# Two matmul stages take the residual times its column weights, and the norm's factor comes at their evictions

## The chip, the cores and the metric

The kernel runs on one core of a Trainium2 chip. The metric is the device time of one execution in microseconds (us), as the median of three runs. A difference of about 0.2% (6 us here) is the least that a measurement of this kernel can tell from none.

## What is computed

Two transformer-like blocks over T = 256 tokens of D = 2048 features. The change is in the last two parts of the second block: a cross attention to 256 memory tokens and a squared-ReLU MLP, each behind an RMS norm of the running sum `h`:

```python
def rmsnorm_2(x, w):
    xf = x.astype(jnp.float32)
    y = xf * lax.rsqrt(jnp.mean(xf * xf, axis=-1, keepdims=True) + RMS_EPS)
    return (y * w.astype(jnp.float32)).astype(x.dtype)

def squared_relu_mlp(u, w1, w2):
    return jnp.square(jax.nn.relu(u @ w1)) @ w2
...
        h = h + jnp.concatenate([o_dn, o_rw], axis=-1).astype(h.dtype) @ w_out[l]
        h = h + memory_cross_attention(rmsnorm_2(h, xa_norm_w[l]), rmsnorm_2(mem, mem_norm_w[l]),
                                       xa_wq[l], xa_wk[l], xa_wv[l], xa_wo[l])
        h = h + squared_relu_mlp(rmsnorm_2(h, ffn_norm_w[l]), ffn_w1[l], ffn_w2[l])
    return rmsnorm_2(h, final_norm_w)
```

The norm's factor, `rsqrt(mean(x²) + eps)`, is one number per token. Everything is float32 in and out.

## The kernel before

**Layout.** Activations stand transposed in SBUF: features on the 128 partitions, 16 feature tiles, and the 256 tokens in the columns. The running sum is `resid`, 16 tiles of 128x256. A token's factor is therefore a column's factor, the same for all partitions; `rs` (128x256) holds it on every partition.

**A gemm.** Weights come from HBM in slabs of 512 KB (four 128-row tiles by 256 columns), in a ring of four slots `raw`. ScalarE (ACT) rounds a slab to `hi` (line 276), VectorE (DVE) subtracts to get the rest, `lo` (line 312), and TensorE (PE) multiplies. For one slab it runs a group of 8 matmuls of `hi` against 512 columns (line 375; the moving operand is `x`'s rounded half and its rest side by side) and 8 of `lo` against 256 (line 382). A gemm's block is 256 output features: with K = 2048 it has four such groups, with K = 1024 two, with K = 512 one. A block's two PSUM halves are evacuated by ACT (`half`, line 286) and DVE (lines 325 to 343, by the gemm's kind), and there are two PSUM buffers, so block b+2 waits for the eviction of block b.

**The order of the work** is written out by hand in one program for each engine. ACT and DVE run one block ahead with the splits: split block b+1, then evacuate block b. `follows` names the next gemm, whose first slabs are split before the last block's eviction. `after(b)` is called behind each block, `each()` behind each slab.

**The stages around the change**, in order, with their blocks and groups per block: `g_ob` (w_out, adds to `resid`, 8 x 2), norm 6, `g_xq` (xa_q, stored in `work`, 2 x 4), the attention (`xat_*`), `g_xo` (xa_o, adds to `resid`, 8 x 1), norm 7, `ff2[0]` (w1_0, 8 x 4), then w2_0, w1_1 and so on to w2_3 (ff2 has four w1 gemms, 32 blocks). The w1 gemms are of kind "relu2": their eviction makes `xb` from relu² in four DVE operations.

**A norm here.** While `g_ob` or `g_xo` runs, ACT squares each finished pair of `resid` tiles (`squares_beside`, line 406), GpSimd (POOL) sums them in `sq_sum` (line 440), and behind the last block two more pairs are squared. Then one PE matmul sums over the partitions (`norm_total`, line 449), ACT makes `rs` (Ln, then a table load and Exp, lines 421 and 422), and DVE and ACT write the 16 tiles of `xa` in turns: `half` = resid x weight x rs on DVE (471), its rounding on ACT (454), the rest on DVE (476). PE's first block of the next gemm waits, group by group, for four tiles each (`x_ready`).

Of the kernel before, what the change touches and what calls it, by code (L numbers as in the profile page):

```python
# [7 lines left out]
F32 = mybir.dt.float32  # L8
# [73 lines left out]
class Gemm:  # L82
# [1 line left out]

    def __init__(self, plan, name, w, k, n0, n, x, kind, dst, x_from=0, bias=None, k0=0, apart=P):
        self.name, self.w, self.n0, self.x, self.kind, self.dst = name, w, n0, x, kind, dst
        self.k0, self.x_from, self.bias, self.apart = k0, x_from, bias, apart
# [43 lines left out]
def build_program(nc, a, out):  # L133
# [3 lines left out]
    with ctx:  # L137
# [10 lines left out]
        def sem(name):  # L148
            return ctx.enter_context(nc.semaphore(name))
# [58 lines left out]
        half_out = sem("half_out")  # L208
        evacuated = sem("evacuated")
        summed = sem("summed")  # L210
        squared, rounded = sem("squared"), sem("rounded")
# [105 lines left out]
        def evacuate(dve, g, i, v):  # L317
            t = i * g.unroll + v
            par = (g.b0 + v) % 2
            into, tile, off = g.dst  # L320
            dve.wait_ge(half_out, g.b0 + t + 1)
            psum = pg[:, par, :, 0:T]
            place = into[:, bass.ds(tile + 2 * t, 2), off:off + T]
            if g.kind == "store":
                nc.vector.tensor_tensor(place, psum, half[:, :, :], ALU.add).then_inc(evacuated, 1)  # L325
                return
            own = g.sum0 + t + 1
            if g.kind in ("add", "mult"):
                nc.vector.tensor_tensor(half[:, :, :], psum, half[:, :, :], ALU.add).then_inc(summed, 1)  # L329
                dve.wait_ge(summed, own)  # L330
                nc.vector.tensor_tensor(place, place, half[:, :, :],  # L331
                                        ALU.add if g.kind == "add" else ALU.mult).then_inc(evacuated, 1)
                return
            own_sq = g.sq0 + t + 1
            nc.vector.tensor_tensor(sq[:, :, :], psum, half[:, :, :], ALU.add).then_inc(summed, 1)
            dve.wait_ge(summed, own)
            nc.vector.scalar_tensor_tensor(out=sq[:, :, :], in0=sq[:, :, :], scalar=0.0, in1=sq[:, :, :],
                                           op0=ALU.max, op1=ALU.mult).then_inc(squared, 1)
# [19 lines left out]
        def gemm_pe(pe, g, after=None, x_tiles=None, of=None, each=None):  # L358
# [30 lines left out]
            if x_tiles is not None or of:  # L389

                for v in range(g.unroll):
                    block(0, v, waits=(v == 0))
                    if after:
                        after(v)
                rest = g.blocks - g.unroll
                run_blocks(pe, rest, g.unroll, lambda i, v: block(i + 1, v),
                           (lambda t: after(t + g.unroll)) if after else None)
            else:
                run_blocks(pe, g.blocks, g.unroll, block, after, each)

# [294 lines left out]
        g_xq = Gemm(plan, "xa_q", a["xa_wq_2"], D, 0, 512, xa, "store", (work, 8, PAD))  # L695
        g_xo = Gemm(plan, "xa_o", a["xa_wo_2"], 512, 0, D, xb, "add", (resid, 0, 0))
        ff2 = []
        for p in range(FF_PIECES):
            ff2 += [Gemm(plan, f"w1_{p}", a["ffn_w1_2"], D, p * D, D, xa, "relu2", (xb, 0, 0)),
                    Gemm(plan, f"w2_{p}", a["ffn_w2_2"], D, 0, D, xb, "add", (resid, 0, 0), k0=p * D)]  # L700

        def over(name, shape, region, byte):
# [1011 lines left out]
        def _(act):  # L1714
# [44 lines left out]
            gemm_act(act, g_ob, squares_beside(act, g_ob, 6, resid, 0, 0), follows=g_xq)  # L1759
            norm_act(act, 6, resid, 0, 0, lambda e, k: blocks_out(e, g_ob), DT - 2)  # L1760
            norm_split_act(act, 4, xa)
            gemm_act(act, g_xq, follows=g_xo)
            xat_act(act)
            gemm_act(act, g_xo, squares_beside(act, g_xo, 7, resid, 0, 0), follows=ff2[0])
            norm_act(act, 7, resid, 0, 0, lambda e, k: blocks_out(e, g_xo), DT - 2)
            norm_split_act(act, 5, xa)
            for g, n in zip(ff2, ff2[1:] + [None]):
                gemm_act(act, g, squares_beside(act, g, 8, resid, 0, 0) if g is ff2[-1] else None, follows=n)
            norm_act(act, 8, resid, 0, 0, lambda e, k: blocks_out(e, ff2[-1]), DT - 2)

        @block.vector
        def _(dve):
# [69 lines left out]
        def _(pe):  # L1842
# [78 lines left out]
```

## Time and profile before

| what | value |
|---|---|
| median of 3 runs | 3098.55 us (3097.56 to 3099.07) |
| the profiled execution: its own time | 3098.79 us |
| its span in the profile | 3097.0 us |
| PE busy | 2885.4 us, 93% |
| DVE busy | 1971.7 us, 64% |
| ACT busy | 1446.5 us, 47% |
| POOL busy | 74.0 us, 2% |
| HBM traffic | 156 GB/s over the span |

The span runs from the first to the last instruction; the execution's own time has 1.8 us around it. Busy shares are means over all stages, so what a change in one stage is worth is read from that stage.

### The profile page before, as it was taken

Reading aid. Unit: us, or ns where it says so; the run is one execution under the profiler, and the core shown is the slowest. Engines: PE = TensorE matmul, PEld = TensorE weight load, DVE = VectorE, ACT = ScalarE, POOL = GpSimd, SP = SyncE. Lnnn points to the kernel's source line nnn. Section 1 sums busy time; section 2 is a strip of 40 time slices with the busy share of each in tenths; the row PEclk is TensorE's granted clock in tenths of the full one; section 3 lists DMA queues with packets and bytes.
Section 4 is the critical chain, followed back from the end, with each engine's and each line's share of the span. In section 5 each row is a group of like instructions: output and inputs, shape, how many; then the busy total and the mean of one; then the engine's idle time right before and its main releaser. Section 6 shows DMA issues by size and latency. Waiting matters only on the chain.

```text
span 3097.0 us, 51788 instructions
## 1 busy us (share of the span) xinstructions
PE 2885.4 (93%) x19568; PEld 2514.7 (81%) x19568; DVE 1971.7 (64%) x2513; ACT 1446.5 (47%) x1866; POOL 74.0 (2%) x90
## 2 busy tenths in 40 slices
PE   6999999979999999997998996887968999999997
PEld 5888888868888888886877885776856888888886
DVE  4588886656556565657865566546657656565665
ACT  4445656554444444445476335325435444444443
POOL 0000000010000000010000000000102000000001
PEclk9999999989999999998999997999988999999999
DMA  5655554636565666653644341013624666666664
GB/s 173 184 186 173 168 172 136 202 114 183 188 186 189 186 190 188 188 186 108 190 155 132 116 123 41 3 43 95 197 75 149 187 188 188 189 186 190 185 192 132
DMA packets 480985, 484.50 MB, mean 156 GB/s; under 512 B 14736, under 2 KB 479632, under 8 KB 480704
## 3 DMA queue, kind: packets, MB, share of 16 engines
q1 hardware_dynamic: 480288, 479.01, 50.0%
q0 software_dynamic: 544, 3.38, 0.3%
q8 instruction: 105, 1.72, 0.2%
q14 instruction: 48, 0.39, 0.0%
HBM read 480.23 MB, written 2.10 MB: 156 GB/s over the span
## 4 chain that ended last, share of the span: by engine, by line
PE 43%; DVE 6%; ACT 3%; issue 1%; POOL 0%; DMA 0%; ACTq 0%; POOLq 0%; DVEq 0%; SPq 0%
PE pg L375 24%; PE pg L382 12%; DVE lo L312 1%; PE p L783 1%; PE p L797 1%; PE p L800 1%; PE p L1156 1%; DVE rw_xx L849 0%; ACT hi L276 0%; PE p L459 0%; POOL sq_sum L440 0%; DVE half L487 0%; DVE dnc L884 0%; PE p L1397 0%; DVE resid L331 0%
## 5 line engine op out<-in xcount | busy, mean ns | idle before, releaser
L312 DVE TENSOR_TENSOR lo<-raw,hi 128x1024 fp32r<-128x1024 f32 x904 | 1100.2, 1231 | 818.4 <-ACT hi L276 814.5
L276 ACT ACTIVATE hi<-raw 128x1024 fp32r<-128x1024 f32 x904 | 947.2, 1058 | 1165.5 <-PE pg L382 1160.3
L375 PE MATMUL pg<-xa,hi 128*128 128x512 f32 x4608 | 1174.7, 397 | 38.7 <-DVE xa L476 37.0
L375 PEld LDWEIGHTS pg<-xa,hi 128*128 128x128 f32 x4608 | 835.9, 190 | 198.9 <-issue 44.4
L375 PE MATMUL pg<-xb,hi 128*128 128x512 f32 x2624 | 664.7, 395 | 10.6 <-DVE xb L579 2.9
L382 PEld LDWEIGHTS pg<-xa,lo 128*128 128x128 f32 x4608 | 631.4, 191 | 46.0
L382 PE MATMUL pg<-xa,lo 128*128 128x256 f32 x4608 | 644.5, 283 | 0.0
L375 PEld LDWEIGHTS pg<-xb,hi 128*128 128x128 f32 x2624 | 475.7, 190 | 99.0 <-ACT hi L276 4.4
L382 PEld LDWEIGHTS pg<-xb,lo 128*128 128x128 f32 x2624 | 358.8, 191 | 28.3 <-DVE lo L312 2.4
L382 PE MATMUL pg<-xb,lo 128*128 128x256 f32 x2624 | 366.7, 283 | 2.0 <-DVE lo L312 2.0
L286 ACT ACTIVATE half<-pg 128x512 f32<-128x512 f32 x212 | 123.7, 583 | 83.8 <-PE pg L382 83.8
L505 DVE SCALAR_TENSOR_TENSOR work<-u,vec,work 128x256 f32<-128x256 f32 x240 | 116.2, 484 | 7.6
L329 DVE TENSOR_TENSOR half<-pg,half 128x512 f32<-128x512 f32 x96 | 65.8, 686 | 41.6 <-ACT half L286 41.3
L459 PE MATMUL p<-sq,cst 128*128 128x256 f32 x128 | 45.3, 487 | 33.1 <-ACT sq L406 32.5
L440 POOL TENSOR_TENSOR sq_sum<-sq_sum,sq 128x256 f32<-128x256 f32 x75 | 67.7, 902 | 204.8 <-ACT sq L406 198.6
L325 DVE TENSOR_TENSOR work<-pg,half 128x512 f32<-128x512 f32 (+1 forms) x88 | 60.2, 684 | 11.9 <-ACT half L286 11.9
L459 PEld LDWEIGHTS p<-sq,cst 128*128 128x128 f32 x128 | 24.0, 227 | 53.3 <-ACT sq L406 29.4
L471 DVE SCALAR_TENSOR_TENSOR half<-resid,vec,rs 128x256 f32<-128x256 f32 x80 | 38.4, 485 | 21.0 <-ACT rs L422 18.5
L454 ACT ACTIVATE xa<-half 128x256 fp32r<-128x256 f32 x80 | 33.3, 417 | 36.2 <-DVE half L471 36.2
L813 ACT ACTIVATE rw_tt<-p 128x256 f32<-128x256 f32 (+1 forms) x48 | 18.4, 384 | 67.0 <-PE p L783 56.5
L343 DVE TENSOR_TENSOR xb<-sq,xb 128x512 f32 (+1 forms) x64 | 44.3, 692 | 7.8 <-DVE xb L340 0.9
L331 DVE TENSOR_TENSOR resid<-resid,half 128x512 f32 (+1 forms) x56 | 42.1, 752 | 5.8 <-DVE half L329 4.9
(364 smaller groups left out, 1649.8 us busy)
## 6 DMA issues: line engine op xcount, KB each, us to landing
raw<-w_in SPq DMA_DIRECT2D x264, 512.0 KB, 4.6
raw<-ffn_w SPq DMA_DIRECT2D x256, 512.0 KB, 4.0
raw<-w_up SPq DMA_DIRECT2D x128, 512.0 KB, 3.9
raw<-w_down SPq DMA_DIRECT2D x128, 512.0 KB, 4.4
raw<-w_o SPq DMA_DIRECT2D x32, 512.0 KB, 4.5
raw<-w_out SPq DMA_DIRECT2D x32, 512.0 KB, 3.5
raw<-w_sb_out SPq DMA_DIRECT2D x16, 512.0 KB, 4.7
raw<-w_conv_out SPq DMA_DIRECT2D x16, 512.0 KB, 4.7
```

The source lines that it names most:

```text
L276: nc.scalar.activation(hi[:, slot], raw[:, slot], ACT.Copy).then_inc(hi_ready, 1)
L286: nc.scalar.activation(half[:, :, :], pg[:, par, :, T:2 * T], ACT.Copy).then_inc(half_out, 1)
L312: nc.vector.tensor_tensor(lo[:, slot], raw[:, slot], hi[:, slot].bitcast(F32), ALU.subtract).then_inc(lo_ready, 1)
L325: nc.vector.tensor_tensor(place, psum, half[:, :, :], ALU.add).then_inc(evacuated, 1)
L329: nc.vector.tensor_tensor(half[:, :, :], psum, half[:, :, :], ALU.add).then_inc(summed, 1)
L331: nc.vector.tensor_tensor(place, place, half[:, :, :], ALU.add if g.kind == "add" else ALU.mult).then_inc(evacuated, 1)
L343: nc.vector.tensor_tensor(rest, sq[:, :, :], place.bitcast(F32), ALU.subtract).then_inc(evacuated, 1)
L375: nc.tensor.matmul(pg[:, par, t, :], lhsT=hi[:, slot, k, c:c + P], rhs=g.x[:, kk, :], start=(j == 0 and k == 0), stop=False)
L382: ins = nc.tensor.matmul(pg[:, par, t, 0:T], lhsT=lo[:, slot, k, c:c + P], rhs=g.x[:, kk, 0:T], start=False, stop=(j == g.groups - 1 and k ...
L440: ins = nc.gpsimd.tensor_tensor(sq_sum[:, :], sq_sum[:, :], sq[:, k % 2], ALU.add)
L459: ins = nc.tensor.matmul(ps[0][:, 0:T], lhsT=const("ones"), rhs=sq[:, k % 2], start=(k == 0), stop=(k == DT - 1))
L505: ins = nc.vector.scalar_tensor_tensor(out=acc, in0=x, scalar=v1("w_dw", 8 * j + c), in1=acc, op0=ALU.mult, op1=ALU.add)
```

## The change

The moving operand of `g_xq` and of the w1 gemms becomes `resid` times its column weights alone. Its two halves are written by one ACT operation (`gained_act`, Copy with the weight as scale) and one DVE operation (`gained_dve`) per tile, beside `g_ob` and `g_xo`: ACT handles tiles 2b-2 and 2b-1 behind block b, DVE tiles 2b-4 and 2b-3, and the last ones behind the gemm (two on ACT; six on DVE, those of block 7 counted). The factor `rs` is applied at the evictions of `g_xq` and of all four w1 gemms, by one DVE operation more per block. PE's sum and ACT's root move into the next gemm: `each()` runs them behind its second slab. GpSimd's and SP's programs stay as they are, and so do the DMAs.

```diff
+            if g.kind == "normed":
+                nc.vector.tensor_tensor(half[:, :, :], psum, half[:, :, :], ALU.add).then_inc(summed, 1)
+                dve.wait_ge(summed, own)
+                norm_rs_dve(dve, g.norm)
+                nc.vector.tensor_tensor(place, half[:, :, :], rs[:, None, :].to_broadcast([P, 2, T]),
+                                        ALU.mult).then_inc(evacuated, 1)
+                return
...
+            if g.norm is None:
+                nc.vector.scalar_tensor_tensor(out=sq[:, :, :], in0=sq[:, :, :], scalar=0.0, in1=sq[:, :, :],
+                                               op0=ALU.max, op1=ALU.mult).then_inc(squared, 1)
+            else:
+                norm_rs_dve(dve, g.norm)
+                nc.vector.scalar_tensor_tensor(out=sq[:, :, :], in0=sq[:, :, :], scalar=0.0,
+                                               in1=rs[:, None, :].to_broadcast([P, 2, T]), op0=ALU.max,
+                                               op1=ALU.mult).then_inc(scaled, 1)
+                dve.wait_ge(scaled, own_sq - ff2[0].sq0)
+                nc.vector.tensor_tensor(sq[:, :, :], sq[:, :, :], sq[:, :, :], ALU.mult).then_inc(squared, 1)
...
+        def gained_act(act, n, m, gain, k):
+            nc.scalar.activation(xa[:, k, 0:T], resid[:, k], ACT.Copy, scale=gain(k)).then_inc(norm_hi, 1)
+            square_tile(act, n, k, resid, 0, 0)
+
+        def gained_beside_act(act, g, n, m, gain):
+
+            def after(b):
+                if b:
+                    act.wait_ge(evacuated, g.b0 + b + 2)
+                    for k in (2 * b - 2, 2 * b - 1):
+                        gained_act(act, n, m, gain, k)
+            return after
+
+        def gained_rest_act(act, g, n, m, gain):
+            act_link(nc.scalar.activation(small[:, 140:141], const("ones")[:, 0:1], ACT.Ln))
+            blocks_out(act, g)
+            for k in (DT - 2, DT - 1):
+                gained_act(act, n, m, gain, k)
+
+        def root_later(act, n):
+            yield
+            norm_root(act, n)
+            yield
+
+        def total_later(pe, n):
+            yield
+            norm_total(pe, n)
+            yield
+
+        def gained_dve(dve, m, gain, k):
+            dve.wait_ge(norm_hi, DT * m + k + 1)
+            nc.vector.scalar_tensor_tensor(out=xa[:, k, T:2 * T], in0=resid[:, k], scalar=gain(k),
+                                           in1=xa[:, k, 0:T].bitcast(F32), op0=ALU.mult,
+                                           op1=ALU.subtract).then_inc(x_ready, 1)
+
+        def gained_beside_dve(dve, m, gain):
+
+            def after(b):
+                if b >= 2:
+                    for k in (2 * b - 4, 2 * b - 3):
+                        gained_dve(dve, m, gain, k)
+            return after
...
-            gemm_act(act, g_xo, squares_beside(act, g_xo, 7, resid, 0, 0), follows=ff2[0])
-            norm_act(act, 7, resid, 0, 0, lambda e, k: blocks_out(e, g_xo), DT - 2)
-            norm_split_act(act, 5, xa)
+            gemm_act(act, g_xo, gained_beside_act(act, g_xo, 7, 5, ffn_gain), follows=ff2[0])
+            gained_rest_act(act, g_xo, 7, 5, ffn_gain)
+            root = root_later(act, 7)
...
-            gemm_dve(dve, g_xo, follows=ff2[0])
-            norm_rs_dve(dve, 7)
-            norm_split_dve(dve, 5, xa, resid, 0, 0, lambda k: v2("ffn_norm_w_2", k), 112)
+            gemm_dve(dve, g_xo, gained_beside_dve(dve, 5, ffn_gain), follows=ff2[0])
+            for k in range(DT - 4, DT):
+                gained_dve(dve, 5, ffn_gain, k)
...
-            norm_total(pe, 7)
-            gemm_pe(pe, ff2[0], x_tiles=112)
+            gemm_pe(pe, ff2[0], x_tiles=112, each=step_of(total_later(pe, 7)))
```

`g_xq` has the same three edits with norm 6.

PE's order at the start of `g_xq`, before; the first row is the norm's sum over partitions, the others are the groups of block 0 (the start of `ff2[0]` reads alike):

```order
L449 MATMUL p<-sq_sum,cst 128x256
L375 MATMUL pg<-xa,hi 128x512 x8
L382 MATMUL pg<-xa,lo 128x256 x8
L375 MATMUL pg<-xa,hi 128x512 x8
L382 MATMUL pg<-xa,lo 128x256 x8
L375 MATMUL pg<-xa,hi 128x512 x8
```

The same place after the change (the lines are now 464, 390 and 397):

```order
L390 MATMUL pg<-xa,hi 128x512 x8
L397 MATMUL pg<-xa,lo 128x256 x8
L390 MATMUL pg<-xa,hi 128x512 x8
L397 MATMUL pg<-xa,lo 128x256 x8
L464 MATMUL p<-sq_sum,cst 128x256
L390 MATMUL pg<-xa,hi 128x512 x8
```

The sum has moved behind two groups of matmuls; PE's queue is in order, so the third group stands behind it.

DVE's order at the end of `g_xo`, before: two blocks, the four splits of w1_0's first slabs, the last eviction, and the start of the turns of norm 7:

```order
L331 TENSOR_TENSOR resid<-resid,half 128x512
L312 TENSOR_TENSOR lo<-raw,hi 128x1024
L329 TENSOR_TENSOR half<-pg,half 128x512
L331 TENSOR_TENSOR resid<-resid,half 128x512
L312 TENSOR_TENSOR lo<-raw,hi 128x1024 x4
L329 TENSOR_TENSOR half<-pg,half 128x512
L331 TENSOR_TENSOR resid<-resid,half 128x512
L471 SCALAR_TENSOR_TENSOR half<-resid,vec,rs 128x256 x2
L476 TENSOR_TENSOR xa<-half,xa 128x256
```

The same place after:

```order
L331 TENSOR_TENSOR resid<-resid,half 128x512
L502 SCALAR_TENSOR_TENSOR xa<-resid,vec,xa 128x256 x2
L312 TENSOR_TENSOR lo<-raw,hi 128x1024
L329 TENSOR_TENSOR half<-pg,half 128x512
L331 TENSOR_TENSOR resid<-resid,half 128x512
L502 SCALAR_TENSOR_TENSOR xa<-resid,vec,xa 128x256 x2
L312 TENSOR_TENSOR lo<-raw,hi 128x1024 x4
L329 TENSOR_TENSOR half<-pg,half 128x512
L331 TENSOR_TENSOR resid<-resid,half 128x512
L502 SCALAR_TENSOR_TENSOR xa<-resid,vec,xa 128x256 x6
```

Two operations of line 502 stand behind the eviction of each block from the third on, and six behind the last one; the 32 operations of lines 471 and 476 are gone.

## Rows read from the trace of the kernel before

**Rows 1.** The page's part 4: the chain that ended last, by engine.

```profile
PE 43%; DVE 6%; ACT 3%; issue 1%; POOL 0%; DMA 0%; ACTq 0%; POOLq 0%; DVEq 0%; SPq 0%
```

**Rows 2.** PE's waits over the whole span: in total us, times, longest.

```profile
PE pg L375 <- DVE xa L476: 37.0, 5, 11.9
...
PE p L449 <- POOL sq_sum L440: 31.7, 5, 8.6
```

**Rows 3.** Timeline, `g_ob` to the attention: start us, us, engine, operation.

```profile
2249.22 4.03 DVE L312 TENSOR_TENSOR lo<-raw,hi 128x1024 fp32r<-128x1024 f32 x3
...
2251.45 1.11 PE L382 MATMUL pg<-xb,lo 128*128 128x256 f32 x8
...
2254.59 4.03 POOL L440 TENSOR_TENSOR sq_sum<-sq_sum,sq 128x256 f32<-128x256 f32 x4 [4.69 <-ACT sq L406]
...
2255.61 0.69 DVE L331 TENSOR_TENSOR resid<-resid,half 128x512 f32<-128x512 f32 x1
...
2258.67 1.22 PE L449 MATMUL p<-sq_sum,cst 128*128 128x256 f32 x2 [6.11 <-POOL sq_sum L440]
...
2262.08 0.88 DVE L471 SCALAR_TENSOR_TENSOR half<-resid,vec,rs 128x256 f32<-128x256 f32 x2 [5.77 <-ACT rs L422]
...
2266.19 3.74 PE L375 MATMUL pg<-xa,hi 128*128 128x512 f32 x8 [6.29 <-DVE xa L476]
...
2287.48 2.00 PE L375 MATMUL pg<-xa,hi 128*128 128x512 f32 x8
...
2291.10 0.69 DVE L325 TENSOR_TENSOR work<-pg,half 128x512 f32<-128x512 f32 x1 [6.63 <-ACT half L286]
```

**Rows 4.** Timeline, `g_xo` to the second block of w1_0.

```profile
2339.86 2.11 PE L375 MATMUL pg<-xb,hi 128*128 128x512 f32 x8
...
2342.86 2.10 PE L375 MATMUL pg<-xb,hi 128*128 128x512 f32 x8
...
2344.80 1.11 PE L382 MATMUL pg<-xb,lo 128*128 128x256 f32 x8
...
2345.65 5.16 DVE L312 TENSOR_TENSOR lo<-raw,hi 128x1024 fp32r<-128x1024 f32 x4
...
2350.37 4.07 POOL L440 TENSOR_TENSOR sq_sum<-sq_sum,sq 128x256 f32<-128x256 f32 x4 [4.05 <-ACT sq L406]
...
2351.45 0.69 DVE L331 TENSOR_TENSOR resid<-resid,half 128x512 f32<-128x512 f32 x1
...
2362.01 3.63 PE L375 MATMUL pg<-xa,hi 128*128 128x512 f32 x8 [6.29 <-DVE xa L476]
...
2374.88 2.00 PE L375 MATMUL pg<-xa,hi 128*128 128x512 f32 x8
```

**Rows 5.** Windows in g_ob, g_xo, w1_0: busy PE, PEld, DVE, ACT, POOL; PEclk.

```profile
2208.00:2252.60 44.60, 44.57 (x256) 39.03 (x254) 33.02 (x32) 24.49 (x37) 10.42 (x12) 1.00 0.53 168
...
2321.30:2345.90 24.60, 24.56 (x128) 20.95 (x128) 19.64 (x22) 15.30 (x27) 11.49 (x12) 0.94 0.44 131
...
2375.00:2455.00 80.00, 80.00 (x458) 70.28 (x457) 52.02 (x58) 34.69 (x37) 0.00 (x0) 1.00 0.65 199
```

**Rows 6.** Groups by form, DVE, 2329:2346, in `g_xo`.

```profile
L312 DVE TENSOR_TENSOR lo<-raw,hi 128x1024 fp32r<-128x1024 f32 x7 | 11.5, 1648 | 0.1
```

**Rows 7.** The page's part 5: the splits of line 312, all of them.

```profile
L312 DVE TENSOR_TENSOR lo<-raw,hi 128x1024 fp32r<-128x1024 f32 x904 | 1100.2, 1231 | 818.4 <-ACT hi L276 814.5
```

**Rows 8.** ACT's operation with a per-partition operand: ns min/median/max.

```profile
L1275 ACT ACTIVATE rw_d<-work,vec x8: 494/496/499, 1881.2 to 1884.0; 128x256 f32<-128x256 f32 x8
```

**Rows 9.** Timeline, PE, at two waits of an earlier stage, norms of `g_dn`.

```profile
1580.29 2.07 PE L917 MATMUL p<-sq,cst 128*128 128x512 f32 x2 [2.68 <-ACT sq L931]
1581.37 3.51 PE L375 MATMUL pg<-xa,hi 128*128 128x512 f32 x8
...
1595.41 1.12 PE L917 MATMUL p<-sq,cst 128*128 128x512 f32 x2 [1.20 <-ACT sq L931]
1596.45 2.06 PE L375 MATMUL pg<-xa,hi 128*128 128x512 f32 x8
```

More of the change, by code:

```diff
@@ L82, with __init__ @@
 class Gemm:
-    def __init__(self, plan, name, w, k, n0, n, x, kind, dst, x_from=0, bias=None, k0=0, apart=P):
+    def __init__(self, plan, name, w, k, n0, n, x, kind, dst, x_from=0, bias=None, k0=0, apart=P, norm=None):
         self.name, self.w, self.n0, self.x, self.kind, self.dst = name, w, n0, x, kind, dst
-        self.k0, self.x_from, self.bias, self.apart = k0, x_from, bias, apart
+        self.k0, self.x_from, self.bias, self.apart, self.norm = k0, x_from, bias, apart, norm
         self.groups = k // (P * KG)
@@ L210, in build_program @@
         summed = sem("summed")
-        squared, rounded = sem("squared"), sem("rounded")
+        squared, rounded, scaled = sem("squared"), sem("rounded"), sem("scaled")
         x_ready = sem("x_ready")
@@ L336, in evacuate @@
             dve.wait_ge(summed, own)
-            nc.vector.scalar_tensor_tensor(out=sq[:, :, :], in0=sq[:, :, :], scalar=0.0, in1=sq[:, :, :],
-                                           op0=ALU.max, op1=ALU.mult).then_inc(squared, 1)
+            if g.norm is None:
[8 more added lines that the diff above has]
+                nc.vector.tensor_tensor(sq[:, :, :], sq[:, :, :], sq[:, :, :], ALU.mult).then_inc(squared, 1)
             dve.wait_ge(squared, own_sq)
@@ L396, in gemm_pe @@
                 run_blocks(pe, rest, g.unroll, lambda i, v: block(i + 1, v),
-                           (lambda t: after(t + g.unroll)) if after else None)
+                           (lambda t: after(t + g.unroll)) if after else None, each)
             else:
@@ L454, in norm_split_act @@
                 nc.scalar.activation(x[:, k, 0:T], tmp[:, k % 2], ACT.Copy).then_inc(norm_hi, 1)
+        def gained_act(act, n, m, gain, k):
[32 more added lines that the diff above has]
+            return after
+        xa_gain, ffn_gain = lambda k: v2("xa_norm_w_2", k), lambda k: v2("ffn_norm_w_2", k)
         def norm_pe(pe, n, k0=0, k1=DT):
@@ L694, in build_program @@
         g_ob = Gemm(plan, "w_out rw", a["w_out_2"], D // 2, 0, D, xb, "add", (resid, 0, 0), x_from=8, k0=D // 2)
-        g_xq = Gemm(plan, "xa_q", a["xa_wq_2"], D, 0, 512, xa, "store", (work, 8, PAD))
+        g_xq = Gemm(plan, "xa_q", a["xa_wq_2"], D, 0, 512, xa, "normed", (work, 8, PAD), norm=6)
         g_xo = Gemm(plan, "xa_o", a["xa_wo_2"], 512, 0, D, xb, "add", (resid, 0, 0))
@@ L698, in build_program @@
         for p in range(FF_PIECES):
-            ff2 += [Gemm(plan, f"w1_{p}", a["ffn_w1_2"], D, p * D, D, xa, "relu2", (xb, 0, 0)),
+            ff2 += [Gemm(plan, f"w1_{p}", a["ffn_w1_2"], D, p * D, D, xa, "relu2", (xb, 0, 0), norm=7),
                     Gemm(plan, f"w2_{p}", a["ffn_w2_2"], D, 0, D, xb, "add", (resid, 0, 0), k0=p * D)]
@@ L1758, in _ @@
             gemm_act(act, g_mv, follows=g_ob)
[L1759 to L1762, printed above, removed]
+            gemm_act(act, g_ob, gained_beside_act(act, g_ob, 6, 4, xa_gain), follows=g_xq)
+            gained_rest_act(act, g_ob, 6, 4, xa_gain)
+            root = root_later(act, 6)
+            gemm_act(act, g_xq, follows=g_xo, each=step_of(root))
             xat_act(act)
-            gemm_act(act, g_xo, squares_beside(act, g_xo, 7, resid, 0, 0), follows=ff2[0])
-            norm_act(act, 7, resid, 0, 0, lambda e, k: blocks_out(e, g_xo), DT - 2)
-            norm_split_act(act, 5, xa)
+            gemm_act(act, g_xo, gained_beside_act(act, g_xo, 7, 5, ffn_gain), follows=ff2[0])
+            gained_rest_act(act, g_xo, 7, 5, ffn_gain)
+            root = root_later(act, 7)
             for g, n in zip(ff2, ff2[1:] + [None]):
-                gemm_act(act, g, squares_beside(act, g, 8, resid, 0, 0) if g is ff2[-1] else None, follows=n)
+                gemm_act(act, g, squares_beside(act, g, 8, resid, 0, 0) if g is ff2[-1] else None, follows=n,
+                         each=step_of(root) if g is ff2[0] else None)
             norm_act(act, 8, resid, 0, 0, lambda e, k: blocks_out(e, ff2[-1]), DT - 2)
@@ L1825, in _ @@
             gemm_dve(dve, g_mv, follows=g_ob)
-            gemm_dve(dve, g_ob, follows=g_xq)
-            norm_rs_dve(dve, 6)
-            norm_split_dve(dve, 4, xa, resid, 0, 0, lambda k: v2("xa_norm_w_2", k), 96)
+            gemm_dve(dve, g_ob, gained_beside_dve(dve, 4, xa_gain), follows=g_xq)
+            for k in range(DT - 4, DT):
+                gained_dve(dve, 4, xa_gain, k)
             gemm_dve(dve, g_xq, follows=g_xo)
             xat_dve(dve)
-            gemm_dve(dve, g_xo, follows=ff2[0])
-            norm_rs_dve(dve, 7)
-            norm_split_dve(dve, 5, xa, resid, 0, 0, lambda k: v2("ffn_norm_w_2", k), 112)
+            gemm_dve(dve, g_xo, gained_beside_dve(dve, 5, ffn_gain), follows=ff2[0])
+            for k in range(DT - 4, DT):
+                gained_dve(dve, 5, ffn_gain, k)
             for g, n in zip(ff2, ff2[1:] + [None]):
@@ L1879, in _ @@
             gemm_pe(pe, g_ob)
-            norm_total(pe, 6)
-            gemm_pe(pe, g_xq, x_tiles=96)
+            gemm_pe(pe, g_xq, x_tiles=96, each=step_of(total_later(pe, 6)))
             blocks_out(pe, g_mv)
```

## The prediction

> **What bounds the kernel now.** I read the chain that ended last first: of the engines PE has by far the largest share [rows 1]. PE's own waits come next, since what PE waits for is what could be won: the norms stand among the largest, with 37.0 us in 5 waits for the first tiles of `xa` and 31.7 us in 5 waits for POOL's sums [rows 2]. Then I read the timeline across the two norms that the change touches.
>
> First gap, `g_ob` to `g_xq` [rows 3]: PE's last group ends at 2251.45 + 1.11 = 2252.56. The last block is in `resid` at 2255.61 + 0.69 = 2256.30, POOL has its last sum at 2254.59 + 4.03 = 2258.62, `rs` lets DVE begin at 2262.08, and PE restarts at 2266.19. That is 13.6 us, and the first `hi` group then takes 3.74 us where the later one takes 2.00.
>
> Second gap, `g_xo` to w1_0 [rows 4]: PE ends at 2344.80 + 1.11 = 2345.91 and restarts at 2362.01, 16.1 us, with a first group of 3.63. Here the stage before is not bound by PE alone: its last blocks start 3.00 us apart (2339.86, 2342.86), while a group takes 44.60 / 16 = 2.79 us in `g_ob` [rows 5] (8 matmuls of each kind per group, 256 records). In that stretch a split of 128x1024 on DVE takes 1.648 us [rows 6] against a mean of 1.231 over the kernel [rows 7], with POOL 11.49 us busy in it, and DVE works 19.64 of 24.60 us [rows 5], the early blocks being looser. So DVE sets the pace of `g_xo`'s second half.
>
> **The change, part by part.** Positions are those of the trace before; I walk each gap anew.
>
> *Beside `g_ob`.* DVE's two new operations per block are like the pair at 2262.08, 0.88 us [rows 3]. DVE is busy 33.02 of 44.60 us, 4.13 per block of 5.58 [rows 5]; 5.0 still fits. ACT gains two copies with a per-partition scale; the nearest row, same shape, is 0.496 us [rows 8]. ACT is busy 24.49 of 44.60, 3.1 per block; 4.1 fits. The cover is PE's 5.58 us; without it the block would cost up to 0.9 us more. I take nothing.
>
> *First gap.* PE runs two groups at once: their tiles 0 to 7 and slabs are ready. It is free at 2252.56 + 5.58 = 2258.14 and comes to the norm's sum. What is late now is POOL. DVE's splits start 0.88 later, at 2250.10, three end at 2254.13 (4.03), the fourth at 2255.36 (1.23), the eviction at 2255.36 + 1.40 = 2256.76 (two operations of 0.69). POOL ended 2.32 after `resid` before; one copy in front of the square makes it 2.82: 2259.6. PE waits 1.4 us, behind it the third group and all after it. The sum itself took 1.22 us before, behind a long idle [rows 3]; at the full clock I halve that to 0.61. These are its bounds, and which of them holds hangs on the clock. The clock: behind an idle 1.20 us the matmuls ran 1.12 and 2.06 us, behind 2.68 us they ran 2.07 and 3.51 [rows 9]. 1.4 is nearer to the first, so I take the full clock: 0.61. Six groups follow from 2260.2: 16.74, to 2276.95. Before, the same point was 2287.48 + 2.79 = 2290.27 [rows 3]. Gain 13.3. `g_xq`'s last eviction gets one multiplication, and the attention waits for it: 0.69 as L325 [rows 3], nothing covers it. **Net 12.6 us.** The factor itself (Ln, table load, Exp on ACT) was ready 2.2 us behind the sum's end before, 2258.67 + 1.22 to 2262.08 [rows 3], so here near 2262.4. The first eviction that needs it comes with block 0's end at 2265.8: hidden. Queued behind the root on ACT is the third `hi` of block 1, which can't start before PE's third group ends at 2263.0 anyway.
>
> *Beside `g_xo`.* DVE has no slack here. Each block from the third on costs 0.88 us. Before the splits of w1_0 there are five such pairs: 4.4 us. PE's first group of w1_0 needs the PSUM of block 6, which is four pairs later.
>
> *Second gap* [rows 4]. The splits start at 2345.65 + 4.4 = 2350.05 and take 5.16: 2355.21. PE's first group waits for the first of them, 2350.05 + 1.65 = 2351.7, ends at 2352.7; the second at 2355.5. The last eviction was done 6.49 us behind the start of the splits (2352.14), so 2356.54. POOL was done 2.30 later (2350.37 + 4.07); with the copy 2.80: 2359.34. PE has then idled 3.9 us, more than the 2.68 of the slow row, so the sum is at the low clock, 1.22: 2360.56. Two groups remain, 5.58, and the slow first one adds 3.63 - 2.00 = 1.63: block 1 starts at 2367.8 instead of 2374.88. **Net 7.1 us.**
>
> *The w1 gemms.* Per block DVE gets one more operation of 0.69 and a link of about 0.15: 0.84, 32 times, 27 us of work. DVE is busy 52.02 of 80.00 us in w1_0, 7.3 of a block's 11.16 [rows 5], so 3.9 are free: nothing. Where w2 begins, its fourth group is the one that needs w1's last eviction, and it comes 8.4 us behind w1's end, with the splits and a 2.5 us eviction in front: the 0.84 is hidden there too. Without that cover the four hand-overs would cost 3.4 us.
>
> *Loops.* PE's and ACT's w1_0 is now written out. No row tells a written-out gemm from a looped one in pace; nothing.
>
> **The sum:** 12.6 + 7.1 = 19.7. From the profiled execution's own 3098.79 (span 3097.0 and 1.8 around it) this gives 3079.1; it stands 0.24 above the median, so 3079 for the median.
>
> **A page against the trace.** In `g_xo` a split beside POOL takes 0.42 us more than the mean [rows 6, 7]; I leave that surcharge as it is, since POOL does the same two additions per block. The Trainium skill, SBUF — State Buffer, section "Who interferes with whom", says that a VectorE instruction with two SBUF inputs and a GpSimd one that reads SBUF exclude each other for the whole instruction. The new operation has two such inputs; read to its end this is rival C. The trace agrees in that the splits stretch, and shows no full blocking of each.
>
> **The rivals.**
> A. The clock falls in the first gap too, if POOL is later by half a microsecond or the clock is quicker to fall than the rows show. Price 0.61 + 1.63 = 2.2: 3081.
> B. It does not fall in the second gap: 3077.
> C. VectorE and GpSimd lock each other out at the new operations. POOL is busy 11.49 / 12 = 0.96 us per addition [rows 5], two per block 1.9, of which 0.42 is paid: 1.5 more. Five blocks of `g_xo`: 7.5, 3086.6. In `g_ob` DVE would need 4.13 + 0.88 + 1.5 = 6.5 of 5.58, another 0.9 in six blocks: 3092. For it: the surcharge. Against: it was 0.42, not 1.9.
> D. It does not close the gaps: if PE's first groups effectively wait for DVE's last tile (2256.76 + six operations of 0.44 = 2259.4; 2359.2 in the second), the gains are about 2290.27 - (2259.4 + 22.3 + 2.2) - 0.7 = 5.7 and 2374.88 - (2359.2 + 11.2 + 2.8) = 1.7: 3091. Against: `x_ready` is asked for four tiles at a time, and tile 7 is written in block 5's turn.
> E. Slower: the w1 evictions become the bound. From the point where the added DVE work per block passes the 3.9 us free, or a lateness of block b reaches PE's block b+2, each of 32 blocks pays 0.84: 27 us against the gain of 19.7, 3106. For it: it is the only part repeated 32 times. Against: the free 3.9.
>
> **How the numbers follow.** Forecast 62% (its own range 3077 to 3082), A 15, B 8, C 8, D 4, E 2, 1 unnamed. The range 3075 to 3086 holds the forecast, A and B and the lower part of C; half a microsecond of POOL either way and a pair at 0.80 to 1.0 us instead of 0.88 move the sum by 2. Faster by over 0.2% (below 3092): forecast, A, B, nearly all of C and D, 0.94. Within 0.2%: the rest of C and D, 0.04. Slower: 0.02.
>
> **What the profile after would show.** First gap: PE's waits for `xa` fall from 5 to 3; one wait of 1 to 2 us for POOL in `g_xq` with the next group at 2.0 to 2.1 us (3.5: rival A). `g_xo`: blocks some 3.9 us apart from the fourth on (over 4.5: C). Second gap: a wait of about 4 us for POOL, then a slow group. w1: DVE busier, groups still 2.79 us apart; any wait of PE for an eviction there speaks for E. The prediction is wrong if the L502 operations take clearly over 0.5 us, or if POOL's last sum comes later than 3 us behind the last eviction.

## The result

The changed kernel takes 3079.84 us as the median of four runs (3077.72 to 3080.55), against 3098.06 for the kernel before on the same chips: a ratio of 0.9941, with a 95% interval of 0.9929 to 0.9954. That is 18.2 us less; 19.7 were forecast, at 3079 in a range of 3075 to 3086.

### The profile page after: what moved, and what is told of

Same layout as the page of the kernel before. It is cut to its first block, busy times and chain, and to the rows that moved or that the text cites. A ratio compares the mean times of both kernels' runs of the same rounds, so it can differ in the third digit from the quotient of the medians.

```text
span 3075.9 us, 51736 instructions
## 1 busy us (share of the span) xinstructions
PE 2884.0 (94%) x19568; PEld 2512.2 (82%) x19568; DVE 1982.4 (64%) x2515; ACT 1446.2 (47%) x1866; POOL 78.4 (3%) x90
## 4 chain that ended last, share of the span: by engine, by line
PE 43%; DVE 6%; ACT 3%; issue 1%; POOL 0%; ACTq 0%; DVEq 0%; POOLq 0%
PE pg L390 24%; PE pg L397 12%; DVE lo L312 1%; PE p L843 1%; PE p L857 1%; PE p L860 1%; PE p L1216 1%; DVE rw_xx L909 0%; ACT hi L276 0%; PE p L519 0%; DVE half L547 0%; DVE resid L331 0%; DVE dnc L944 0%; DVE half L329 0%; PE p L1457 0%
## 5 line engine op out<-in xcount | busy, mean ns | idle before, releaser
L390 PEld LDWEIGHTS pg<-xb,hi 128*128 128x128 f32 x2624 | 475.4, 190 | 100.2 <-ACT hi L276 5.3
L421 ACT ACTIVATE sq<-resid 128x256 f32<-128x256 f32 x96 | 38.5, 411 | 16.3 <-PE p L519 8.9
L331 DVE TENSOR_TENSOR resid<-resid,half 128x512 f32<-128x512 f32 (+1 forms) x56 | 41.5, 741 | 5.0 <-DVE half L329 3.9
L342 DVE TENSOR_TENSOR sq<-pg,half 128x512 f32<-128x512 f32 x64 | 43.8, 684 | 0.0
```

What stands on the lines that cost most here:

```text
L390: nc.tensor.matmul(pg[:, par, t, :], lhsT=hi[:, slot, k, c:c + P], rhs=g.x[:, kk, :], start=(j == 0 and k == 0), stop=False)
```

## The profile after

The profiled execution of the changed kernel is the fastest of its four (3077.72, span 3075.9). PE's waits over the whole span, in total, times and longest, which answer to [rows 2]:

```profile
PE pg L390 <- DVE xa L536: 24.5, 3, 11.9
PE p L464 <- POOL sq_sum L455: 22.1, 5, 6.1
```

The waits for tiles of `xa` have gone from 5 to 3, and the rest are those of other norms. The waits for POOL are still 5, but shorter.

The timeline from the end of `g_ob` to the attention, which answers to [rows 3]:

```profile
2248.36 4.62 DVE L312 TENSOR_TENSOR lo<-raw,hi 128x1024 fp32r<-128x1024 f32 x4
...
2249.05 1.12 PE L397 MATMUL pg<-xb,lo 128*128 128x256 f32 x8
...
2253.62 0.69 DVE L331 TENSOR_TENSOR resid<-resid,half 128x512 f32<-128x512 f32 x1
2254.23 3.88 DVE L502 SCALAR_TENSOR_TENSOR xa<-resid,vec,xa 128x256 fp32r<-128x256 f32 x6
...
2255.66 1.77 POOL L455 TENSOR_TENSOR sq_sum<-sq_sum,sq 128x256 f32<-128x256 f32 x2 [0.76 <-ACT sq L421]
...
2257.48 0.70 PE L464 MATMUL p<-sq_sum,cst 128*128 128x256 f32 x2 [1.73 <-POOL sq_sum L455]
...
2257.83 2.20 PE L390 MATMUL pg<-xa,hi 128*128 128x512 f32 x8
...
2276.33 0.69 DVE L338 TENSOR_TENSOR work<-half,rs 128x512 f32<-128x512 f32 x1
...
2277.17 5.38 PE L1692 MATMUL p<-work 128*128 128x256 f32 x16 [2.23 <-DVE work L338]
...
2282.59 2.29 DVE L1724 TENSOR_REDUCE small<-p 128x8 f32<-128x2048 f32 x1 [5.56 <-PE p L1692]
```

Read it from PE. `g_ob` ends at 2249.05 + 1.12 = 2250.17, and two groups of `g_xq` follow at once. PE then waits 1.73 us for POOL, whose last addition ends at 2255.66 + 1.77 = 2257.43, 3.1 us behind the last eviction (2254.31). The sum takes 0.70 us and the next group 2.20: the clock stayed up, as forecast. At the end stands something that was not forecast: the attention's 16 score records take 5.38 us. In the kernel before, the same row, behind the eviction that ends [rows 3], was:

```profile
2291.94 3.69 PE L1632 MATMUL p<-work 128*128 128x256 f32 x16 [1.50 <-DVE work L325]
```

The windows of these two rows, the changed kernel's first; the third number from the end is the granted clock:

```profile
2277.17:2282.55 5.38, 5.38 (x18) 4.37 (x19) 0.00 (x0) 0.00 (x0) 0.00 (x0) 0.68 0.00 0
2291.94:2295.63 3.69, 3.69 (x18) 3.23 (x19) 0.00 (x0) 0.00 (x0) 0.00 (x0) 1.00 0.00 0
```

PE waited 2.23 us for them instead of 1.50, because `g_xq`'s eviction has one operation more (L338), and they run 1.7 us longer: 1.00 is TensorE's full clock, 2.4 GHz, and part of the 5.38 us ran at its lower level of 1.2.

The same for `g_xo` and w1_0, which answers to [rows 4]:

```profile
2308.26 3.68 PE L390 MATMUL pg<-xb,hi 128*128 128x512 f32 x8 [2.65 <-DVE xb L1737]
...
2318.71 1.27 DVE L312 TENSOR_TENSOR lo<-raw,hi 128x1024 fp32r<-128x1024 f32 x1 [0.94 <-ACT hi L276]
...
2328.91 2.09 PE L390 MATMUL pg<-xb,hi 128*128 128x512 f32 x8 [0.19 <-DVE resid L331]
...
2332.64 2.11 PE L390 MATMUL pg<-xb,hi 128*128 128x512 f32 x8 [0.19 <-DVE resid L331]
...
2337.44 4.62 DVE L312 TENSOR_TENSOR lo<-raw,hi 128x1024 fp32r<-128x1024 f32 x4
...
2342.70 0.69 DVE L331 TENSOR_TENSOR resid<-resid,half 128x512 f32<-128x512 f32 x1
...
2344.38 1.73 POOL L455 TENSOR_TENSOR sq_sum<-sq_sum,sq 128x256 f32<-128x256 f32 x2 [0.40 <-ACT sq L421]
...
2346.16 1.22 PE L464 MATMUL p<-sq_sum,cst 128*128 128x256 f32 x2 [3.44 <-POOL sq_sum L455]
...
2346.82 3.35 PE L390 MATMUL pg<-xa,hi 128*128 128x512 f32 x8
...
2350.94 2.00 PE L390 MATMUL pg<-xa,hi 128*128 128x512 f32 x8
...
2353.74 2.00 PE L390 MATMUL pg<-xa,hi 128*128 128x512 f32 x8
```

`g_xo`'s late blocks start 3.73 us apart (2328.91, 2332.64) instead of 3.00: DVE's two new operations per block cost 0.73 net. Ahead of the first such pair DVE also starts a split late (2318.71, 10.45 us behind the first row; 9.50 before): the new copies on ACT had pushed that slab's `hi` back. The splits of w1_0 start 29.18 us behind the first row, 4.9 us later than before. PE waits 3.44 us for POOL, runs the sum with the next group 0.66 us behind its start, and that group is slow (3.35 us; 4.12 to the next start instead of 2.79). Block 1 of w1_0 is the last row, 2353.74.

DVE's new operation over the whole kernel (ns, minimum/median/maximum), and then the windows of `g_ob`, `g_xo` and w1_0, which answer to [rows 5]:

```profile
L502 DVE SCALAR_TENSOR_TENSOR xa<-resid,vec,xa x32: 470/950/968, 2224.2 to 2346.7; 128x256 fp32r<-128x256 f32 x32
```

```profile
2208.00:2250.00 42.00, 42.00 (x243) 36.96 (x242) 35.33 (x40) 26.89 (x47) 11.75 (x12) 1.00 0.56 175
2308.30:2337.40 29.10, 27.40 (x133) 21.71 (x134) 23.18 (x31) 21.01 (x40) 13.91 (x12) 0.94 0.39 118
2356.50:2436.50 80.00, 80.00 (x458) 70.32 (x457) 56.60 (x66) 34.19 (x36) 0.00 (x0) 1.00 0.60 186
```

The operation takes 0.95 us in the middle, twice what I had assumed, though in `g_xo` only one of each pair does; the sum was still right to a microsecond, and the experiments show why. In w1_0 DVE has gone from 52.0 to 56.6 us of 80, and PE has no gap in it.

To compare profiled executions I cut each trace at four marks on PE, the same in every kernel: the end of `g_ob`, the first score, the first group of `g_xo`, and the start of w1_0's block 1. What lies ahead of the first mark differs between executions although the programs are alike there: the changed kernel's is 2.4 us shorter (2252.56 to 2250.17), which is why its span is 21.1 us shorter and its median only 18.2.

| kernel | median us (before, same chip) | end of g_ob to scores | scores to g_xo | g_xo to block 1 of w1_0 | sum |
|---|---|---|---|---|---|
| before | 3098.06 | 39.38 | 29.40 | 53.54 | 122.3 |
| changed | 3079.84 (3098.06) | 27.00 | 31.09 | 45.48 | 103.6 |
| e1_xq_only | 3087.72 (3097.21) | 26.98 | 31.09 | 53.76 | 111.8 |
| e2_w1_only | 3089.91 (3097.21) | 39.38 | 29.40 | 45.19 | 114.0 |
| e4_store_xq | 3078.62 (3097.21) | 26.27 | 29.17 | 46.81 | 102.3 |
| e5_transposes_first | 3076.10 (3097.21) | 26.90 | 29.29 | 43.98 | 100.2 |
| e7_w1_no_factor | 3078.79 (3098.63) | 26.98 | 31.09 | 45.48 | 103.6 |
| e6_pool_fills | 3077.88 (3098.63) | 26.23 | 32.12 | 43.73 | 102.1 |
| e3_sum_late | 3073.29 (3098.63) | 25.20 | 29.40 | 43.94 | 98.5 |
| e8_both | 3073.51 (3098.63) | 25.13 | 27.74 | 42.40 | 95.3 |
| e9_late_and_sooner | 3068.98 (3098.06) | 25.00 | 27.71 | 40.17 | 92.9 |
| e10_all_three | 3067.87 (3098.06) | 24.92 | 27.74 | 40.16 | 92.8 |

From the last mark to the end all twelve take 722.0 to 722.3 us. The medians of e4 to e7 differ from the changed kernel's by less than the 6 us that a measurement can tell from none. Of the variants e3 to e10 only e9 and e10 have an interval of the ratio to the kernel before that lies clear of the changed kernel's 0.9929 to 0.9954; those of e3 (0.9907 to 0.9934) and e8 (0.9906 to 0.9933) just meet it. What the smaller steps are worth is read from the marks, which are one execution each.

## The experiments

**Each half alone.** In e1_xq_only norm 7 and the w1 gemms go back to the old form:

```diff
-            gemm_pe(pe, ff2[0], x_tiles=112, each=step_of(total_later(pe, 7)))
+            norm_total(pe, 7)
+            gemm_pe(pe, ff2[0], x_tiles=112)
```

> Only g_xq takes the weighted residual (norm 6 as in the changed kernel, norm 7 and the w1 gemms as before). The theory from the changed kernel's trace: the first gap is worth 12.4 us between the end of g_ob and the attention's first matmul, and 1.7 us of it is given back because those matmuls run 5.38 us instead of 3.69. So 10.7 us under the kernel before, near 3087.4. Rival: the two gaps are not independent, the greater part comes from the w1 side and from the loops written out there; then this run is less than 8 us under the kernel before, over 3090.

In e2_w1_only norm 6 and `g_xq` do:

```diff
-            gemm_pe(pe, g_xq, x_tiles=96, each=step_of(total_later(pe, 6)))
+            norm_total(pe, 6)
+            gemm_pe(pe, g_xq, x_tiles=96)
```

> Only the w1 gemms take the weighted residual (norm 7 as in the changed kernel, norm 6 and g_xq as before). The theory: the trace puts 8.1 us on this part, against 7.1 in the prediction; near 3090.0, with the attention's first matmuls at 3.7 us as before. Rival: 7.1 or less was right and the rest is spread between executions, 3091 or more. With the other half the two gains add up to 18 to 19 us.

Measured: 9.5 us under the kernel before (0.9968, 0.9955 to 0.9980) and 7.3 us under it (0.9976, 0.9966 to 0.9985). Together 16.8 against 18.2 for both. The marks add up more closely: 10.5 and 8.4 us, against 18.7. So the two parts add up, within what the executions of one kernel differ by, the first gap is worth more than the second, and the first part brings its slow scores along (31.09 in the second column).

**Whose are the slow scores?** e4_store_xq evicts `g_xq` without the factor:

```diff
-        g_xq = Gemm(plan, "xa_q", a["xa_wq_2"], D, 0, 512, xa, "normed", (work, 8, PAD), norm=6)
+        g_xq = Gemm(plan, "xa_q", a["xa_wq_2"], D, 0, 512, xa, "store", (work, 8, PAD))
```

> The changed kernel, with g_xq evicted by the one addition as before: the factor of norm 6 is left out of the result, and one DVE operation of 0.69 us goes from each of its two evictions. Theory: PE's idle time before the attention falls from 2.2 to 1.5 us, its clock then stays up, the 16 records of the scores take 3.7 instead of 5.4 us, and the run is 0.7 + 1.7 = 2.4 us under the changed kernel, 3077.4. Rival: the slow scores come from the wait for POOL inside g_xq or from chance; then they stay near 5.4 us and the run is only 0.7 us under, 3079.1.

PE's timeline, the scores and then `g_xo`'s first and fourth group:

```profile
2277.83 3.69 PE L1692 MATMUL p<-work 128*128 128x256 f32 x16 [1.50 <-DVE work L325]
...
2307.00 3.78 PE L390 MATMUL pg<-xb,hi 128*128 128x512 f32 x8 [2.65 <-DVE xb L1737]
...
2318.71 2.11 PE L390 MATMUL pg<-xb,hi 128*128 128x512 f32 x8 [0.26 <-ACT hi L276]
```

Waiting 1.50 us, the scores are at full pace again (granted clock 1.00), and the first two columns are 2.65 us shorter. The last one gave 1.3 us back in this execution (46.81 instead of 45.48), since `g_xo` began with a longer slow stretch: from its first to its fourth group 11.7 us, against 10.5 in the changed kernel. The median is 1.2 us under the changed kernel's, with intervals that overlap. The place is shown by the trace, the size of it in the median is not settled.

e5_transposes_first keeps the factor and gives PE work to do meanwhile:

```diff
-            blocks_out(pe, g_xq)
-            for h in range(XA_H):
...
-            XA_.pe.done(ins, "s")
+            pe.wait_ge(evacuated, g_xq.b0 + 3)
             for n in range(8):
                 ins = nc.tensor.transpose(pgq(0)[:, n], chunk(4 + n // 2, n % 2), const("ident"))
             XA_.pe.done(ins, "v")
+            blocks_out(pe, g_xq)
+            for h in range(XA_H):
...
+            XA_.pe.done(ins, "s")
```

> The changed kernel, with the attention's eight transposes of v put ahead of the scores, so that PE has 1.04 us of work while g_xq's last eviction runs. Theory of the clock by idle time: PE idles some 1.2 us before the scores, they take 3.7 us, and with the transposes out of the way the run is up to 1.7 us under the changed kernel (DVE waits for the scores alone, so hiding the transposes gives nothing by itself), 3078.1. Rival: eight short transposes don't keep the clock, the scores stay at 5.4 us and the run is the same as the changed kernel, 3079.8.

PE's rows, transposes, scores, and the first group of `g_xo`:

```profile
2276.27 1.04 PE L1691 MATMUL pg<-cst,work 128*128 128x128 f32 x8
2278.57 3.72 PE L1696 MATMUL p<-work 128*128 128x256 f32 x16 [1.26 <-DVE work L338]
...
2307.86 2.10 PE L390 MATMUL pg<-xb,hi 128*128 128x512 f32 x8 [2.65 <-DVE xb L1738]
```

The scores are at full pace behind 1.26 us, as expected. The last row was not expected: behind the same 2.65 us of waiting as in all other kernels so far, that group took 2.10 us, not 3.5 to 3.8. The marks are 3.4 us shorter, the sum of both (1.8 in the second column, 1.5 in the third). The median is 3.7 us under the changed kernel's, 2.0 more than the forecast of up to 1.7; the intervals of the ratios overlap (0.9918 to 0.9945 here).

**Where the sum stands.** e3_sum_late moves PE's sum and ACT's root two slabs further:

```diff
         def total_later(pe, n):
             yield
+            yield
+            yield
             norm_total(pe, n)
```

and the same in `root_later`.

> The changed kernel, with PE's sum over partitions behind the fourth group of the next gemm's first block instead of the second, and ACT's root behind the fourth split. Theory: PE's waits for POOL (1.73 us in g_xq, 3.44 us in w1_0) are the price of where the sum stands. Without them the first gap loses 1.8 us more; in the second PE next waits for tile 11, which DVE writes 2 us behind the end of the second group, so that 2.2 us of the wait go, and the slow third group (3.35 us) falls back to 2.0 to 2.1: 3.5 together. 5.3 us under the changed kernel, 3074.5. Rival: what ends the wait is DVE's tiles all along, and moving the sum changes nothing, 3079.8; or the late factor holds up the evictions and the run is slower.

PE's timeline around `g_xq`, and then in w1_0:

```profile
2261.42 0.60 PE L464 MATMUL p<-sq_sum,cst 128*128 128x256 f32 x2
...
2275.42 3.69 PE L1696 MATMUL p<-work 128*128 128x256 f32 x16 [2.23 <-DVE work L338]
```

```profile
2304.82 3.62 PE L390 MATMUL pg<-xb,hi 128*128 128x512 f32 x8 [2.65 <-DVE xb L1741]
...
2341.33 2.66 PE L390 MATMUL pg<-xa,hi 128*128 128x512 f32 x8 [2.09 <-DVE xa L506]
...
2348.52 0.60 PE L464 MATMUL p<-sq_sum,cst 128*128 128x256 f32 x2
```

No wait for POOL is left at either place; the next wait is the forecast one for tile 11 (2.09 us). The median is 6.5 us under the changed kernel's, the marks give 5.0, and 5.3 were expected, but not where they came: 1.8 us in the first column, as expected, 1.7 in the second, where the scores ran 3.69 us although PE had again waited 2.23 for them, and only 1.5 of 3.5 in the third, where the group behind the wait was still slow (2.66). So the length of the wait alone does not decide the clock: over these scores the granted clock was 1.00, against 0.68 in the changed kernel.

**Two further steps.** e8_both joins the late sum and the transposes.

> The late sum and the transposes of v ahead of the scores together. If the two act at different places they add up: the late sum's 5.3 us and the 3.7 us that the transposes gave (1.7 by the scores' clock, the rest by the first group of g_xo, which ran 2.10 instead of 3.68 us): 3071 to 3073. If the clock of later matmuls depends on what PE did before, they do not add up, 3074 or more.

Its profiled execution was 3069.83 and has a fast first group in `g_xo`, but the other four are 3072.5 to 3074.0, and the median, 3073.51, is that of the late sum alone within 0.3 us and lies between the two forecasts. What the transposes bring there is not in every execution, and this row of the table (95.3) flatters the kernel.

e9_late_and_sooner lets DVE write its tiles one block earlier at both norms, on top of the late sum (the lines of norm 7):

```diff
-                if b >= 2:
-                    for k in (2 * b - 4, 2 * b - 3):
+                if b >= 1:
+                    for k in (2 * b - 2, 2 * b - 1):
                         gained_dve(dve, m, gain, k)
...
-            for k in range(DT - 4, DT):
+            for k in range(DT - 2, DT):
                 gained_dve(dve, 5, ffn_gain, k)
```

> The late sum, and DVE writes tiles 2b-2 and 2b-1 behind block b instead of 2b-4 and 2b-3, so that four operations instead of six stand behind the last eviction. Theory: with the sum late, PE's next wait in w1_0 is the 2.09 us for tile 11; it goes, the third group is back at full pace (2.66 to 2.0 us), and what then ends last is tile 15, moved by one more pair ahead of the splits (+0.7) and two operations fewer behind the last eviction (-1.3): 1 to 1.5 us under the late sum alone, near 3072. Rival: ACT's copies are not there yet when DVE asks for them beside g_xo, so that each block waits, and it is slower than the late sum alone (over 3074).

PE's rows: scores, first group of `g_xo`, and w1_0's fourth group with the one wait left there:

```profile
2276.99 3.69 PE L1696 MATMUL p<-work 128*128 128x256 f32 x16 [2.23 <-DVE work L338]
...
2304.70 2.11 PE L390 MATMUL pg<-xb,hi 128*128 128x512 f32 x8 [2.65 <-DVE xb L1741]
...
2341.75 2.08 PE L390 MATMUL pg<-xa,hi 128*128 128x512 f32 x8 [1.06 <-DVE xa L506]
```

The median is 3068.98, 4.3 us under the late sum alone, where 1 to 1.5 were forecast. In w1_0 the wait of 2.09 for tile 11 is gone, the third group runs in 2.00 us, and what ends last is tile 15, with a wait of 1.06: the mechanism that was expected. The third column is 3.8 us shorter, of which this part makes 2.3. The other part is clock and was not forecast, 1.5 us at the first group of `g_xo` and 1.7 at the matmuls in front of it (27.71 instead of 29.40 in the second column).

e10_all_three adds the transposes to that.

> Late sum, sooner tiles and transposes first. The two runs with the late sum had one and the same median with and without the transposes; so the theory now is that the transposes give something only where the scores would run at the low clock, as in the changed kernel, and nothing where they run at the full one: the same as the run without them within 1 us, near 3072. Rival: the kept clock at the first group of g_xo (2.10 instead of 3.6 us) is worth its 1.5 us in every execution: near 3070.5.

The three stretches agree with e9's within 0.1 us, so there is no sign that the transposes give anything where the scores run at full pace anyway. The forecast time, near 3072, missed, since e9 itself was 3 us faster than that. Its 3067.87 is the lowest time of the study (ratio 0.9902, 0.9885 to 0.9918), 30 us under the kernel before, and not to be told from e9.

**Why the operation of 0.95 us did not cost more.** e6_pool_fills takes POOL's reads away beside DVE:

```diff
-                    ins = nc.gpsimd.tensor_tensor(sq_sum[:, :], sq_sum[:, :], sq[:, k % 2], ALU.add)
+                    if n in (6, 7):
+                        ins = nc.gpsimd.memset(sq_sum[:, :], 1.0)
+                    else:
+                        ins = nc.gpsimd.tensor_tensor(sq_sum[:, :], sq_sum[:, :], sq[:, k % 2], ALU.add)
```

> The changed kernel, with POOL's additions for norms 6 and 7 replaced by fills of the same tile that read nothing (the sums of squares are left out of the result). Theory: DVE's new operation (0.95 us in the middle, 0.47 at the least) is slow because it meets POOL's reads. Then all 32 take 0.48 us, the splits in g_xo stay at 1.22, g_xo's blocks come 3.4 to 3.5 us apart instead of 3.73, POOL's tail behind the last eviction is shorter by about 0.5 us, and the run is 1.5 to 3 us under the changed kernel, 3077 to 3078. Rival: the operation is slow by itself (three operands, output in fp32r); then it stays at 0.95 us and the run at 3079.8.

DVE's groups by form in `g_xo`, 2320 to 2337, of the changed kernel and then 2322 to 2337 of this one (count, busy us, mean ns):

```profile
L502 DVE SCALAR_TENSOR_TENSOR xa<-resid,vec,xa 128x256 fp32r<-128x256 f32 x9 | 6.4, 742 | 0.0
L312 DVE TENSOR_TENSOR lo<-raw,hi 128x1024 fp32r<-128x1024 f32 x4 | 4.8, 1212 | 0.0
```

```profile
L312 DVE TENSOR_TENSOR lo<-raw,hi 128x1024 fp32r<-128x1024 f32 x5 | 6.1, 1220 | 0.0
L505 DVE SCALAR_TENSOR_TENSOR xa<-resid,vec,xa 128x256 fp32r<-128x256 f32 x10 | 4.4, 479 | 0.0
```

Without POOL's additions the new operation takes 0.479 us, so it is the meeting with POOL that makes it slow, and not its operands. And in the changed kernel the splits have fallen to 1.212 us from the 1.648 of [rows 6]. Which operation pays is seen in one block of `g_xo`, before and after: one of POOL's additions, DVE's operation beside it, and, after, the addition beside the next split:

```profile
2342.15 1.17 POOL L440 TENSOR_TENSOR sq_sum<-sq_sum,sq 128x256 f32<-128x256 f32 x1
2342.65 1.75 DVE L312 TENSOR_TENSOR lo<-raw,hi 128x1024 fp32r<-128x1024 f32 x1
```

```profile
2328.19 1.18 POOL L455 TENSOR_TENSOR sq_sum<-sq_sum,sq 128x256 f32<-128x256 f32 x1
2328.70 0.95 DVE L502 SCALAR_TENSOR_TENSOR xa<-resid,vec,xa 128x256 fp32r<-128x256 f32 x1
...
2330.25 1.53 POOL L455 TENSOR_TENSOR sq_sum<-sq_sum,sq 128x256 f32<-128x256 f32 x1 [0.88 <-ACT sq L421]
```

The one that starts second is the long one. Before, the split began while an addition ran and took 1.75 us. Now the first operation of the pair stands in that place and takes 0.95; the second takes 0.48; and the split begins 0.28 us ahead of the next addition (2329.97) and keeps its 1.21, while the addition takes 1.53. Over both norms of the changed kernel, the 21 new operations that began while an addition ran took 0.94 to 0.97 us and the other 11 took 0.47 to 0.48. So the pair occupies DVE for 1.27 us (2328.70 to 2329.97), the split has become 0.54 shorter, and the block costs 1.27 - 0.54 = 0.73 us more.

In e6 `g_xo`'s late blocks come 3.26 us apart, less than the 3.4 to 3.5 that were forecast. Its median is 2.0 us under the changed kernel's, inside the forecast 1.5 to 3, with intervals that overlap; the marks give 1.5, with a second column 1.0 us longer, where the granted clock was lower (0.68 against 0.73).

**The factor at 32 evictions.** e7_w1_no_factor:

```diff
-        ... xa, "relu2", (xb, 0, 0), norm=7),
+        ... xa, "relu2", (xb, 0, 0)),
```

> The changed kernel, with the w1 evictions as they were before (the factor of norm 7 is left out of the result), which takes one DVE operation of 0.69 us from each of 32 blocks. Theory: PE never waits for these evictions, so nothing changes, 3079.8 within 1 us, and PE's waits in that stretch stay as they are. Rival: the operation costs something at the hand-overs to w2 or in each block; then the run is up to 3.4 us (four hand-overs) or up to 27 us (all blocks) under the changed kernel.

The marks are the changed kernel's to 0.02 us, and DVE's load in w1_0 falls back from 56.6 to 52.3 us of 80. All evictions of w1 come behind the last mark, and the stretch from there to the end settles them: 722.13 us before, 722.14 in the changed kernel, 722.12 here. PE has one wait in it in each of the three, 4.9 us for POOL at the final norm. The median is 1.0 us lower, within the executions' spread. The factor in the w1 gemms costs nothing that can be measured.

## Why the prediction was right, and where it was off

- **Beside `g_ob`: nothing.** Right. DVE is busy 35.3 of 42.0 us there, and PE without a gap.
- **First gap, net 12.6.** By the marks 12.4 up to the first score. POOL ended 3.1 us behind the last eviction, not 2.8, and PE waited 1.73 instead of 1.4; the clock stayed up, rival A did not come. Two misses cancel in front of it: DVE's last splits began 0.65 us later than forecast (1.81 instead of 2.46 us ahead of PE's end), and splits and hand-over to the eviction took 4.54 instead of 5.26.
- **"`g_xq`'s last eviction gets one multiplication ... 0.69 ... nothing covers it."** This is the term that was too small. The operation cost its 0.7, and behind PE's longer wait the clock fell under the scores, 1.7 us more in the profiled execution (second column). With a wait of 1.51 us or less the scores ran at full pace in all six profiles (before, e2, e4, e5, e8, e10), with 2.23 us in two of six; so the longer wait made the loss possible and did not bring it every time. I had put the rows on idle time beside the sum's wait and not beside this one.
- **Beside `g_xo`, 0.88 per block, 4.4 in all.** 0.73 per block, and 4.9 in all. The size is in part luck: I took 0.88 for the pair and left the split at its slow 1.65, and measured were 1.27 for the pair and 0.54 less for the split. The late split behind ACT's copies makes 0.95 us of the 4.9; the prediction weighed ACT beside `g_ob` only.
- **Rival C, and "no full blocking".** Its mechanism is real, without its price. An operation that starts second waits for most of what is left of the addition, about half a microsecond, and not for a whole one; that is how a surcharge of 0.4 on the splits went with an addition of 0.96.
- **The signs of failure.** Both appeared: operations clearly over 0.5 us (0.95), and POOL's last sum more than 3 us behind the last eviction (3.1 in the first gap, 2.7 in the second). The time was right all the same, so both were badly chosen.
- **Second gap, net 7.1.** 8.1. From the start of the splits to block 1 it took 16.3 us and not 17.7: PE waited 3.44 and not 3.9, the sum held the next group up for 0.66 and not 1.22 us, and the slow group cost 1.33 instead of 1.63; the 0.5 lost beside `g_xo` goes off again. The clock fell as forecast, rival B did not come.
- **w1 evictions: nothing.** Right (e7); rival E is out. Rival D too: PE's first two groups ran at once in both places.
- **The sum.** 12.4 - 1.7 + 8.1 = 18.8 by the marks, 18.2 by the medians, 19.7 forecast. The path was right. That the total came within 1.5 us is in part luck, since the errors of -1.7 and +1.0 stand against each other.

## What to carry to other kernels

A factor that is one number per column commutes with the matmul: take it out of the operand, and the gemm starts without it; its price is one operation per eviction, free wherever the evicting engine has slack and dear only at the last eviction in front of a dependent stage. When an in-order queue gets such a late reduction, ask where its input ends and put it behind that: here two groups later were worth 5.0 us by the marks and 6.5 by the medians, beside the 18 of the change itself. When VectorE meets GpSimd's reads, ask which operation starts second, since that one paid in every block looked at here. Count every new wait of PE against its clock, not only the ones inside the edit.

## What the runs showed of the hardware

- VectorE's 128x256 operation with two SBUF inputs takes 0.48 us by itself and 0.94 to 0.97 when it begins while a GpSimd addition runs; the 128x1024 one takes 1.21 and, in that place, 1.75. Where the VectorE operation began first it kept its time, and the addition took 1.53 us. The Trainium skill, SBUF — State Buffer, section "Who interferes with whom", has GpSimd and a VectorE instruction with two SBUF inputs exclude each other when GpSimd reads; the trace agrees in that the one that starts second waits for most of what is left of the first (about 0.5 of 0.67 us). Fills, which read nothing, leave 0.48 us: in e6 nine operations saw a fill start beside them and one began while a fill ran. The other 22 met none, so this part rests on ten.
- The length of a wait does not tell the clock behind it. Behind 2.23 us the scores ran 5.38 us in the changed kernel, e1, e6 and e7 (granted clock 0.68 in the changed kernel), and 3.69 in e3 and e9 (1.00). Behind 2.65 us the first group of `g_xo` took 3.5 to 3.8 us in eight profiles (0.53 in the changed kernel) and 2.1 in four (e5, e8, e9, e10; 1.00 in e5 and e9). Behind 1.73 us or less none of these places was slow. What else decides was not found; each such place is worth 1.5 to 1.7 us, and the executions of one program differ by as much.
